# Two expert layers: how their last rows are added, branched past, normalised and stored, and where one weight bundle waits

## The chip, the core and the metric

One core of a Trainium2 chip runs the whole program. The metric is the device time of one execution in microseconds; the median of 3 executions counts. All values are f32; large products are made of fp32r halves (a value is cut into a high part and what is left of it, "hi" and "lo", and three products of halves are summed).

## What is computed

A first block (gated delta rule plus dilated attention, then a feed-forward layer) is followed by a second block of two layers, each of attention and a mixture of experts. S = 256 rows of D = 1024 values. What the change touches, from the reference:

```python
for i in range(DEPTH_2):                      # two layers
    mod = silu_c @ ada_w[i] + ada_b[i]        # modulation: shifts, scales and gates from c
    sh1, sc1, g1, sh2, sc2, g2 = [m[:, None, :] for m in jnp.split(mod, 6, axis=-1)]
    h = rms_norm(x, norm_mix_g[i]) * (1.0 + sc1) + sh1
    ...                                       # attention of the layer; x = x + g1 * y
    h = rms_norm(x, norm_ffn_g[i]) * (1.0 + sc2) + sh2
    x = x + g2 * grouped_moe(h, router_w, router_bias, moe_w_gate[i], moe_w_up[i], moe_w_down[i])
return x

def grouped_moe(...):                         # 16 experts, top 2 of one group of 4
    for e in range(N_EXPERTS):
        he = jax.nn.silu(t @ w_gate[e]) * (t @ w_up[e])
        out = out + gates[:, e:e + 1] * (he @ w_down[e])
```

## The kernel before, in words

The program is written by hand for each engine, with semaphores between them. The rows x (x_res) lie as 2 tiles (t) of 128 rows x 1024 columns; a half is 512 columns, one PSUM bank.

**An expert layer.** The experts go in 8 pairs (p). For a pair, up to 64 rows for each expert are gathered by a product with a 0/1 matrix; then come 4 gate units and 4 up units (`pair_up`, L1230), each with 1 MB of weights, SiLU on ScalarE (L1378), a product on VectorE (`hid_mul`, L1479), four transposes (L1303), a copy (`hid_copy`, L1482), and 4 down units (`pair_down`, L1240). VectorE scales the two result halves into o_f (`out_rows`, L1428), ScalarE copies them as fp32r into o_hi (`out_hi`, L1368), VectorE takes the difference o_lo (`out_lo`, L1433), and TensorE scatters: for each tile and half, sel_t times o_hi and o_lo into a bank (`scatter_mm`, L632), which VectorE adds to x (`add_rows`, L1464). The scatter of a pair runs within the next pair, behind its transposes. For pairs 0, 2, 4 and 6 it has only banks 0 and 1, so its third and fourth part wait until the first and second are added.

**The last pair** makes its down products by halves (`last_down_pe`): half 0 of all four units, then half 1; each half then goes through out_rows, out_hi, out_lo, scatter and add (`last_out_dve`, `last_scatter_pe`, `last_scatter_dve`).

**The overflow branch.** If an expert has more than 64 rows, further rounds run in a loop. Each engine loads a flag into a register (TENSOR_LOAD) and branches past the loops; in these runs they are skipped. The branch stands behind the last scatter on TensorE, behind the last add on VectorE.

**Between the layers.** In layer 0 ScalarE loads the Sqrt table, makes the high parts of two bundles of the next QKV weights (`splits`, L618), squares x with a row sum (L739) and takes the root (L708). VectorE makes the low parts (L622), the reciprocal (L757) and two scaled identities (`norm_apply`, L765). TensorE turns and scales the rows by 16 f32 products (`turn_pe`, L803); VectorE applies the modulation (`shift_dve`, L853), ScalarE and VectorE cut the result into a_hi (L844) and a_lo (L858), four pieces in order; then the QKV products run (L632), one weight bundle per piece of two column blocks.

**The end.** SP stores the two tiles of x, 512 KB each, when each is complete (L1761).

**Order of transfers.** SP issues weight loads in program order into a ring of 17 places (`PLACE_ORDER`); place 17 is made of last_place and grow. POOL issues the 48 bundles of the modulation weights (ada_w), each 1 MB with a place from a table (`ADA_PLACE`); TensorE multiplies them one by one (`ada_bundle`, L557). Ahead of layer 0's QKV products stand bundles 40, 41 and 42, with filler products (`busy`, L1207: f32 128x128 products whose result is not read) of 8, 5 and 0 behind them (`BUSY_MOD`).

## Time and profile before

| what | value |
|---|---|
| time, median of 3 runs | 1154.24 us (1153.57 to 1154.55) |
| profiled execution, its own time | 1153.23 us |
| its span, first to last instruction | 1151.3 us |
| TensorE busy | 1100.7 us (96%) |
| VectorE, ScalarE, GpSimd busy | 603.7, 423.7, 101.0 us |
| mean granted TensorE clock | 0.995 of full |

Times within the profile are microseconds from the start of the span. A row of the timeline has start, duration, engine, line, operation, out<-in and how many instructions were merged; in brackets stands how long the engine was idle ahead of it, and what released it. PE is TensorE's products, PEld its weight loads, DVE VectorE, ACT ScalarE. A plain f32 product leaves two records: the 17 fillers at the program's start (L1864) show as 34.

### The profile page before, as it was taken

Reading aid. Unit: us, or ns where it says so; the run is one execution under the profiler, and the core shown is the slowest. Engines: PE = TensorE matmul, PEld = TensorE weight load, DVE = VectorE, ACT = ScalarE, POOL = GpSimd, SP = SyncE. Lnnn points to the kernel's source line nnn. Section 1 sums busy time; section 2 is a strip of 40 time slices with the busy share of each in tenths; the row PEclk is TensorE's granted clock in tenths of the full one; section 3 lists DMA queues with packets and bytes.
Section 4 is the critical chain, followed back from the end, with each engine's and each line's share of the span. In section 5 each row is a group of like instructions: output and inputs, shape, how many; then the busy total and the mean of one; then the engine's idle time right before and its main releaser. Section 6 shows DMA issues by size and latency. Waiting matters only on the chain.

```text
span 1151.3 us, 17400 instructions
## 1 busy us (share of the span) xinstructions
PE 1100.7 (96%) x6870; PEld 744.2 (65%) x6870; DVE 603.7 (52%) x1164; ACT 423.7 (37%) x731; POOL 101.0 (9%) x193
## 2 busy tenths in 40 slices
PE   9999999999999999999999999987999999999986
PEld 9887667899999967777634434326888754343422
DVE  3588756767887765676423322327756522332223
ACT  6445434644444444474401202106547412020200
POOL 0211123111121120020000000002000100000000
PEclk9999999999999999999999999998999999999999
DMA  9987684997999878665899999996576789999995
GB/s 289 299 254 275 219 319 143 262 341 216 329 332 305 259 257 308 208 232 175 335 399 409 409 409 408 410 402 221 176 264 239 281 300 409 409 409 409 409 409 232
DMA packets 164910, 356.14 MB, mean 309 GB/s; under 512 B 10840, under 2 KB 79704, under 8 KB 164704
## 3 DMA queue, kind: packets, MB, share of 16 engines
q1 hardware_dynamic: 147792, 295.81, 71.0%
q0 software_dynamic: 17024, 59.26, 15.0%
q8 instruction: 50, 0.82, 0.3%
q14 instruction: 28, 0.23, 0.1%
q10 hardware_dynamic: 16, 0.02, 0.0%
HBM read 351.89 MB, written 7.36 MB: 312 GB/s over the span
## 4 chain that ended last, share of the span: by engine, by line
PE 77%; DMA 9%; DVE 7%; ACT 3%; SPq 2%; issue 1%; POOL 0%; POOLq 0%; DVEq 0%; ACTq 0%
PE bank L632 38%; PE bank L1230 15%; PE bank L1240 8%; DMA ering<-in_moe_w_up 3%; DMA work<-in_moe_w_up 3%; PE bank L1199 3%; PE bank L557 2%; DMA ering<-in_ada_w 1%; PE bank L803 1%; PE bank L937 1%; SPq L502 1%; DVE wlo L622 1%; PE bank L2020 1%; PE bank L1303 1%; PE bank L968 1%
## 5 line engine op out<-in xcount | busy, mean ns | idle before, releaser
L622 DVE TENSOR_TENSOR wlo<-wraw,whi 128x1024 fp32r<-128x1024 f32 x150 | 179.1, 1221 | 58.3 <-ACT whi L618 57.6
L618 ACT ACTIVATE whi<-wraw 128x1024 fp32r<-128x1024 f32 x150 | 153.8, 1052 | 57.1 <-PE bank L632 51.7
L632 PE MATMUL bank<-a_hi,whi 128*128 128x256 f32 x512 | 146.3, 286 | 0.4 <-DVE wlo L622 0.3
L632 PE MATMUL bank<-a_lo,whi 128*128 128x256 f32 x512 | 144.8, 283 | 0.0
L632 PE MATMUL bank<-a_hi,wlo 128*128 128x256 f32 x512 | 144.8, 283 | 0.0
L1230 PE MATMUL bank<-ering,work 128*64 128x512 f32 x528 | 118.5, 595 | 6.0 <-DMA ering<-in_moe_w_gate 4.3
L1479 DVE TENSOR_TENSOR work<-work,bank 128x512 f32<-128x512 f32 x16 | 11.0, 687 | 197.7 <-PE bank L1230 197.7
L1368 ACT ACTIVATE o_hi<-work 128x512 fp32r<-128x512 f32 x32 | 20.2, 631 | 231.5 <-DVE work L1428 231.1
L632 PE MATMUL bank<-whi,a_hi 128*128 128x512 f32 x256 | 104.1, 407 | 0.8 <-DVE wlo L622 0.8
L632 PEld LDWEIGHTS bank<-a_hi,whi 128*128 128x128 f32 x512 | 98.0, 191 | 9.5 <-issue 7.3
L632 PE MATMUL bank<-whi,a_lo 128*128 128x512 f32 x256 | 99.9, 390 | 0.0
L632 PE MATMUL bank<-wlo,a_hi 128*128 128x512 f32 x256 | 99.8, 390 | 0.0
L632 PEld LDWEIGHTS bank<-a_lo,whi 128*128 128x128 f32 x512 | 98.1, 192 | 0.7
L632 PEld LDWEIGHTS bank<-a_hi,wlo 128*128 128x128 f32 x512 | 98.1, 192 | 0.0
L1230 PEld LDWEIGHTS bank<-ering,work 128*64 128x64 f32 x528 | 36.8, 137 | 81.6 <-issue 69.3
L1428 DVE SCALAR_TENSOR_TENSOR work<-bank,sm,mrow 128x512 f32<-128x512 f32 x32 | 22.7, 747 | 87.6 <-PE bank L1240 87.6
L632 PEld LDWEIGHTS bank<-whi,a_hi 128*128 128x128 f32 x256 | 48.1, 188 | 16.5 <-issue 6.6
L1356 ACT ACTIVATE work<-bank,mcol 128x256 f32<-128x256 f32 x64 | 31.8, 561 | 70.5 <-PE bank L1199 70.5
L632 PEld LDWEIGHTS bank<-whi,a_lo 128*128 128x128 f32 x256 | 48.1, 188 | 10.3
L632 PEld LDWEIGHTS bank<-wlo,a_hi 128*128 128x128 f32 x256 | 48.2, 188 | 8.8 <-issue 0.2
L1240 PE MATMUL bank<-ering,work 128*64 128x512 f32 x240 | 53.5, 595 | 0.0
L1464 DVE TENSOR_TENSOR x_res<-x_res,bank 128x512 f32<-128x512 f32 x64 | 40.2, 680 | 9.0 <-PE bank L632 9.0
(349 smaller groups left out, 1931.4 us busy)
## 6 DMA issues: line engine op xcount, KB each, us to landing
ering<-in_moe_w_gate SPq DMA_DIRECT2D x36, 1024.0 KB, 18.5
ering<-in_moe_w_up SPq DMA_DIRECT2D x30, 1024.0 KB, 14.6
ering<-in_moe_w_down SPq DMA_DIRECT2D x30, 1024.0 KB, 18.4
work<-in_ada_w POOLq DMA_DIRECT2D x44, 512.0 KB, 7.5
ering<-in_ada_w POOLq DMA_DIRECT2D x38, 512.0 KB, 5.4
wraw<-in_w_in SPq DMA_DIRECT2D x28, 512.0 KB, 7.2
work<-in_moe_w_up SPq DMA_DIRECT2D x14, 1024.0 KB, 16.4
work<-in_moe_w_down SPq DMA_DIRECT2D x14, 1024.0 KB, 18.0
```

What stands on the lines that cost most here:

```text
L502: sp.dma_start(dst, src).then_inc(raw_in[c % RING], 16)
L557: mm = nc.tensor.matmul(psum[ADA_BANK[g]][32 * q:32 * q + 32, :], silc[:, k, :], ada_part(n, q // 2)[:, (q % 2) * HALF:(q % 2 + 1) * HALF] ...
L618: nc.scalar.activation(w_hi(c), wraw[:, c % RING, :], ACT.Copy).then_inc(w_hi_done, 1)
L622: nc.vector.tensor_tensor(w_lo(u[0]), wraw[:, u[0] % RING, :], w_hi(u[0]).bitcast(F32), ALU.subtract).then_inc(w_lo_done, 1)
L632: mm = nc.tensor.matmul(out_ap, l, r, start=first and n == 0, stop=last and n == len(terms) - 1)
L1199: mm = nc.tensor.matmul(bank[:, kk * S:kk * S + cols], part[:, t, pair_cols(2 * b + kk)], sel[:, t, 0:cols // PAIR_SLOTS, :], start=n == 1 ...
L1230: mm = nc.tensor.matmul(bank[rows, :], x_e[:, k, rows], eunit(r, e)[:, kk * HALF:(kk + 1) * HALF], start=first and kk == 0, stop=last and ...
L1240: mm = nc.tensor.matmul(psum[4 + half][rows, :], hid_t[:, m % 4, rows], eunit(r, e)[:, half * HALF:(half + 1) * HALF], start=first, stop=last)
L1356: ins = nc.scalar.activation(xe[:, :, k, :], gather_bank(g, b)[:, kk * S:(kk + 1) * S].rearrange("p (a c) -> p a c", a=2), ACT.Identity, b ...
L1368: nc.scalar.activation(o_hi[:, cols], o_f[:, cols], ACT.Copy).then_inc(e_o_hi, 1)
L1428: return nc.vector.scalar_tensor_tensor(out=o_f[:, cols], in0=psum[4 + half][:, :], scalar=sm[:, M_GS:M_GS + 1], in1=mrow[:, 1, cols], op0 ...
L1464: return nc.vector.tensor_tensor(xs, xs, scatter_bank(p, n)[:, :], ALU.add)
```

## The change

It has six parts. (1) In the last two pairs the second half of each row tile is added in PSUM: within the last pair's up products, behind its second up unit, TensorE writes x's second halves into banks 6 and 7 by two f32 products with the identity, and the scatters of pairs 6 and 7 accumulate onto them. Pair 6 no longer waits for adds. VectorE copies the two banks into x at the end. (2) The last pair's second half is scattered from o_f by plain f32 products, without o_hi and o_lo. (3) The overflow branch stands ahead of the last pair's down products on TensorE, and ahead of the last `out_rows` on VectorE and `out_hi` on ScalarE. (4) Behind layer 0 the row sums are taken by halves, the second halves directly from the banks; one QKV bundle instead of two is cut ahead of them, three low parts are made within the modulation loop, and 10 fillers follow the last scatter on TensorE. (5) The result is stored in quarters of 256 KB, two by SP and two by ScalarE's queue. (6) Modulation bundle 42 goes into place 17 long before its use (POOL issues it behind `mod_spread(0)`), instead of the place in work.

```diff
+LAST_TWO = (PAIRS - 2, PAIRS - 1)
...
+BUSY_NEXT = 10
...
-ADA_TAIL = [0, 1, 2, 0, 1, 2, 11, 12, 14, 15, 13, 16, 2, 13, 16, 2]
+ADA_TAIL = [0, 1, 2, 0, 1, 2, 11, 12, 14, 15, 17, 16, 2, 13, 16, 2]
...
+ADA_EARLY = 42
...
+            return {11: 3, 12: 4, 13: 5, 14: 0, 15: 1, 16: 0, 17: 6}.get(ADA_PLACE[n], ADA_PLACE[n])
...
+            if at == 17:
+                return place_unit(LAST_PLACE, h)
...
+        def store_quarter(eng, n):
+
+            rows_, cols = slice(n % T * P, (n % T + 1) * P), slice(n // T * HALF, (n // T + 1) * HALF)
+            eng.wait_ge(x_done, X_AT["moe", 1] - X_W + n + 1)
+            eng.dma_start(out[0, rows_, cols], x[:, n % T, cols]).then_inc(x_rows, 16)
...
+        def norm_sums_of_halves(act):
+
+            for t in range(T):
+                act.wait_ge(x_done, X_AT["moe", 0] - X_W + t + 1)
+                nc.scalar.activation(hn[:, t, 0:HALF], x[:, t, 0:HALF], ACT.Square,
+                                     accum_out=sm[:, M_MS + t:M_MS + t + 1]).then_inc(nrm_sq, 1)
+            act.wait_ge(nrm_sq, 2 * 5 + 2)
+            nc.scalar.activation(sm[:, M_MS:M_MS + T], sm[:, M_MS:M_MS + T], ACT.Identity, bias=sm[:, M_EPS:M_EPS + 1],
+                                 scale=1.0 / D).then_inc(nrm_sq, 1)
+            for t in range(T):
+                act.wait_ge(e_sct, 4 * PAIRS - T + t + 1)
+                nc.scalar.activation(hn[:, t, HALF:D], psum[6 + t][:, :], ACT.Square,
+                                     accum_out=sm[:, M_SS + t:M_SS + t + 1]).then_inc(nrm_sq, 1)
+            act.wait_ge(nrm_sq, 2 * 5 + 5)
+            for t in range(T):
+                ins = nc.scalar.activation(sm[:, M_RS + t:M_RS + t + 1], sm[:, M_SS + t:M_SS + t + 1], ACT.Sqrt,
+                                           bias=sm[:, M_MS + t:M_MS + t + 1], scale=1.0 / D)
+            ins.then_inc(nrm_rs, 1)
 
...
+                    behind(b)
...
+            if p in LAST_TWO:
+                return psum[(0, 6, 1, 7)[n]]
+            if p < 0 or p % 2:
                 return psum[(0, 1, 6, 7)[n]]
             return psum[n % 2]
 
         def scatter_mm(p, n):
 
             t, half = n // 2, n % 2
+            on_rows = p in LAST_TWO and half == 1
             return products(scatter_bank(p, n)[:, :], [(sel_t[:, t, :], part[:, half * HALF:(half + 1) * HALF])
-                                                       for part in (o_hi, o_lo)], True, True)
+                                                       for part in (o_hi, o_lo)], not on_rows, not on_rows)
+
+        def rows_into_banks():
+
+            for t in range(T):
+                mm = nc.tensor.matmul(psum[6 + t][:, :], ident, x[:, t, HALF:D], start=True, stop=False)
+            return mm
+
+        def split_rows(l, p, half):
+
+            return 2 * turn_of(l, p) - l + half + 1
 
         def scatter_pe(pe, l, p, part):
 
             q = turn_of(l, p)
             if part == 0:
-                pe.wait_ge(e_o_lo, 2 * (q + 1))
+                pe.wait_ge(e_o_lo, split_rows(l, p, 1))
                 pe.wait_ge(e_sel_t, q + 1)
             for n in (2 * part, 2 * part + 1):
-                if part and p % 2 == 0:
+                if part and p % 2 == 0 and p not in LAST_TWO:
                     pe.wait_ge(x_done, X_AT["wo", l] + X_W * p + n - 1)
                 scatter_mm(p, n).then_inc(e_sct, 1)
...
+                    if p == PAIRS - 1 and kind == 1 and j == 1:
+                        pe.wait_ge(x_done, X_AT["wo", l] + X_W * (PAIRS - 2))
+                        rows_into_banks()
...
             q = turn_of(l, PAIRS - 1)
             pe.wait_ge(e_sel_t, q + 1)
-            for half in range(2):
-                pe.wait_ge(e_o_lo, 2 * q + half + 1)
-                for t in range(T):
-                    scatter_mm(PAIRS - 1, 2 * t + half).then_inc(e_sct, 1)
+            pe.wait_ge(x_done, X_AT["moe", l] - X_W)
+            pe.wait_ge(e_o_lo, split_rows(l, PAIRS - 1, 0))
+            for t in range(T):
+                scatter_mm(PAIRS - 1, 2 * t).then_inc(e_sct, 1)
+            pe.wait_ge(e_o, 2 * (q + 1))
+            for t in range(T):
+                nc.tensor.matmul(psum[6 + t][:, :], sel_t[:, t, :].bitcast(F32), o_f[:, HALF:D], start=False,
+                                 stop=True).then_inc(e_sct, 1)
...
-                dve.wait_ge(e_o_hi, 2 * q + half + 1)
-                out_lo(half).then_inc(e_o_lo, 1)
+                if half == 0:
+                    dve.wait_ge(e_o_hi, split_rows(l, PAIRS - 1, 0))
+                    out_lo(0).then_inc(e_o_lo, 1)
...
-            for n in range(4):
+            for n in range(0, 4, 2 if p in LAST_TWO else 1):
                 dve.wait_ge(e_sct, 4 * turn_of(l, p) + n + 1)
-                add_rows(p, n).then_inc(x_done, 1)
-
-        def last_scatter_dve(dve, l):
-
-            for i, n in enumerate((0, 2, 1, 3)):
-                dve.wait_ge(e_sct, 4 * turn_of(l, PAIRS - 1) + i + 1)
-                add_rows(PAIRS - 1, n).then_inc(x_done, 1)
+                add_rows(p, n).then_inc(x_done, 2 if p in LAST_TWO else 1)
+
+        def rows_from_bank(t):
+            return nc.vector.tensor_copy(x[:, t, HALF:D], psum[6 + t][:, :])
+
+        def last_scatter_dve(dve, l, splits_dve):
+
+            for t in range(T):
+                dve.wait_ge(e_sct, 4 * turn_of(l, PAIRS - 1) + t + 1)
+                add_rows(PAIRS - 1, 2 * t).then_inc(x_done, 1)
+            if l == 0:
+                splits_dve(U_QKV[1] + 1)
+            for t in range(T):
+                if l == 0:
+
+                    dve.wait_ge(nrm_sq, 2 * 5 + 4 + t)
+                else:
+                    dve.wait_ge(e_sct, 4 * turn_of(l, PAIRS - 1) + T + t + 1)
+                rows_from_bank(t).then_inc(x_done, 1)
 
...
-                            sp.wait_ge(mod_rows, 256)
+                            sp.wait_ge(ada_used, ada_count(ADA_EARLY))
...
-            for t in range(T):
-                sp.wait_ge(x_done, X_AT["moe", 1] - (T - 1 - t))
-                sp.dma_start(out[0, t * P:(t + 1) * P, :], x[:, t, :]).then_inc(x_rows, 16)
-            sp.wait_ge(x_rows, 16 * (T + 1))
+            for n in range(0, 2 * T, 2):
+                store_quarter(sp, n)
+            sp.wait_ge(x_rows, 16 * (2 * T + 1))
...
+            pool.wait_ge(mod_rows, 256)
+            load_ada(pool, ADA_EARLY)
...
+                if l == 1:
+                    busy(psum[2], BUSY_NEXT)
...
-                last_scatter_pe(pe, l)
                 over = pe.value_load(ints[0:1, 0:1], min_val=0, max_val=1)
                 with pe.If(over > 0):
-                    pe.drain().then_inc(ov_pe[l], OV_PE)
-                    for r in range(1, ROUNDS):
-                        with pe.Fori(0, PAIRS) as i:
-                            over_pe(pe, l, r, i)
+                    over_begin_pe(pe, l)
+                    with pe.Fori(0, PAIRS * (ROUNDS - 1)) as i:
+                        over_pe(pe, l, 1, i)
                     over_end(pe, l)
+                    rows_into_banks()
+                last_down_pe(pe, l)
+                last_scatter_pe(pe, l)
 
 
 
...
-                out_hi(act, l, PAIRS - 1)
...
+                out_hi(act, l, PAIRS - 1, (0,))
+                if l == 0:
+
                     act.wait_ge(e_used, TURNS)
-                    splits(U_QKV[1] + 2)
+                    splits(U_QKV[1] + 1)
+            for n in range(1, 2 * T, 2):
+                store_quarter(act, n)
...
-                shift_dve(dve, 3 + 3 * l, mcol[:, l, 0:8], mcol[:, l, 8:16])
+                shift_dve(dve, 3 + 3 * l, mcol[:, l, 0:8], mcol[:, l, 8:16],
+                          lambda b: splits(U_QKV[1] + b + 1) if l == 1 and b < 4 else None)
...
-                last_out_dve(dve, l)
-                last_scatter_dve(dve, l)
                 dve.wait_ge(table_done, l + 1)
                 over = dve.value_load(ints[0:1, 0:1], min_val=0, max_val=1)
                 with dve.If(over > 0):
...
                     over_end(dve, l)
-                if l == 0:
-                    splits(U_QKV[1] + 2)
+                last_out_dve(dve, l)
+                last_scatter_dve(dve, l, splits)
```

What moves on the engines, as the instruction lists show it. o_hi and o_lo are the fp32r halves of a pair's result, sel_t the scatter matrix, work the f32 result o_f or weights. TensorE at the end of the second expert layer, before, behind the last down product:

```order
L1240 MATMUL bank<-a_raw_56,work 64x512 [waits first_in]
L1240 MATMUL bank<-a_raw_56,work 64x512
L632 MATMUL bank<-o_hi,sel_t 128x512 [waits e_o_lo,e_sel_t]
L632 MATMUL bank<-o_lo,sel_t 128x512
L632 MATMUL bank<-o_hi,sel_t 128x512
L632 MATMUL bank<-o_lo,sel_t 128x512
L632 MATMUL bank<-o_hi,sel_t 128x512 [waits e_o_lo]
L632 MATMUL bank<-o_lo,sel_t 128x512
L632 MATMUL bank<-o_hi,sel_t 128x512
L632 MATMUL bank<-o_lo,sel_t 128x512
L2263 TENSOR_LOAD ints
```

After, from the last unit's down products to the program's end:

```order
L1270 MATMUL bank<-work 64x512 x4
L1270 MATMUL bank<-a_raw_55,work 64x512 x2
L1270 MATMUL bank<-a_raw_56,work 64x512 [waits first_in]
L1270 MATMUL bank<-a_raw_56,work 64x512
L643 MATMUL bank<-o_hi,sel_t 128x512 [waits e_o_lo,x_done,e_sel_t]
L643 MATMUL bank<-o_lo,sel_t 128x512
L643 MATMUL bank<-o_hi,sel_t 128x512
L643 MATMUL bank<-o_lo,sel_t 128x512
L1395 MATMUL bank<-work,sel_t 128x512 [waits e_o]
```

Four fp32r products and the flag's load are gone from behind the last down products, and two plain f32 products stand there. The flag's load now stands ahead of the down products, here from within pair 6's scatter on (L1317 turns sel_g; the x_res row behind the branch is skipped):

```order
L643 MATMUL bank<-o_hi,sel_t 128x512
L643 MATMUL bank<-o_lo,sel_t 128x512
L643 MATMUL bank<-o_hi,sel_t 128x512
L643 MATMUL bank<-o_lo,sel_t 128x512
L643 MATMUL bank<-o_hi,sel_t 128x512
L643 MATMUL bank<-o_lo,sel_t 128x512
L1317 MATMUL bank<-con,work 128x128 [waits e_sel_t,e_sel_g]
L1317 MATMUL bank<-con,work 128x128
L2368 TENSOR_LOAD ints [waits e_o,e_hid_t]
L2368 ISA x2
L2369 COMPARE_AND_BRANCH
```

VectorE behind layer 0, from the branch to the second piece of the modulation, before:

```order
L3034 UNCONDITIONAL_BRANCH [waits ov_dve0]
L622 TENSOR_TENSOR wlo<-wraw,whi 128x1024 [waits w_hi_done] x2
L757 RECIPROCAL sm<-sm 128x2 [waits nrm_rs]
L765 TENSOR_SCALAR hn<-con,sm 128x128 [waits nrm_inv]
L765 TENSOR_SCALAR hn<-con,sm 128x128
L853 TENSOR_SCALAR work<-bank,mcol 128x256 [waits tr_done]
L853 TENSOR_SCALAR work<-bank,mcol 128x256
L853 TENSOR_SCALAR work<-bank,mcol 128x256 [waits tr_done]
L853 TENSOR_SCALAR work<-bank,mcol 128x256
L858 TENSOR_TENSOR a_lo<-work,a_hi 128x512 [waits a_hi_done]
L853 TENSOR_SCALAR work<-bank,mcol 128x256 [waits tr_done]
```

The same stretch after, from the last pair's `out_rows` of half 1 on:

```order
L1477 SCALAR_TENSOR_TENSOR work<-bank,sm,mrow 128x512 [waits e_used]
L1514 TENSOR_TENSOR x_res<-x_res,bank 128x512 [waits e_sct] x2
L633 TENSOR_TENSOR wlo<-wraw,whi 128x1024 [waits w_hi_done]
L1523 COPY x_res<-bank 128x512 [waits nrm_sq] x2
L786 RECIPROCAL sm<-sm 128x2 [waits nrm_rs]
L794 TENSOR_SCALAR hn<-con,sm 128x128 [waits nrm_inv]
L794 TENSOR_SCALAR hn<-con,sm 128x128
L882 TENSOR_SCALAR work<-bank,mcol 128x256 [waits tr_done]
L882 TENSOR_SCALAR work<-bank,mcol 128x256
L882 TENSOR_SCALAR work<-bank,mcol 128x256 [waits tr_done]
L882 TENSOR_SCALAR work<-bank,mcol 128x256
L887 TENSOR_TENSOR a_lo<-work,a_hi 128x512 [waits a_hi_done]
```

The branch has moved up, out of this stretch; two of four adds became copies that wait for ScalarE's squares (nrm_sq); one of two low parts (wlo) went into the modulation loop.

## Rows read from the trace of the kernel before

**Rows 1.** The page: the chain that ended last, shares by engine.

```profile
PE 77%; DMA 9%; DVE 7%; ACT 3%; SPq 2%; issue 1%; POOL 0%; POOLq 0%; DVEq 0%; ACTq 0%
```

**Rows 2.** Timeline, layer 0's end, TensorE's products.

```profile
763.03 1.94 PE L1230 MATMUL bank<-work 128*64 128x512 f32 x8 [0.62 <-DMA work<-in_moe_w_up]
...
767.79 0.50 PE L632 MATMUL bank<-o_hi,sel_t 128*128 128x512 f32 x1 [0.46 <-DVE x_res L1464]
...
769.26 1.94 PE L1240 MATMUL bank<-work 128*64 128x512 f32 x8
```

**Rows 3.** The same timeline, a later window.

```profile
776.51 0.50 PE L632 MATMUL bank<-o_hi,sel_t 128*128 128x512 f32 x1
...
777.32 0.40 PE L632 MATMUL bank<-o_lo,sel_t 128*128 128x512 f32 x1
...
785.02 5.33 PE L803 MATMUL bank<-hn,x_res 128*128 128x128 f32 x32 [5.00 <-DVE hn L765]
```

**Rows 4.** Timeline, layer 0's last down products, TensorE's weight loads.

```profile
770.70 0.14 PEld L1240 LDWEIGHTS bank<-a_raw,work 128*64 128x64 f32 x2 [0.38 <-DMA a_raw<-in_moe_w_down]
...
772.07 0.20 PEld L1240 LDWEIGHTS bank<-a_raw,work 128*64 128x64 f32 x4 [0.89 <-DMA a_raw<-in_moe_w_down]
```

**Rows 5.** Timeline, layer 0's end, VectorE.

```profile
776.63 0.75 DVE L1428 SCALAR_TENSOR_TENSOR work<-bank,sm,mrow 128x512 f32<-128x512 f32 x1 [1.22 <-PE bank L1240]
...
778.69 2.47 DVE L1464 TENSOR_TENSOR x_res<-x_res,bank 128x512 f32<-128x512 f32 x4
781.52 2.36 DVE L622 TENSOR_TENSOR wlo<-wraw,whi 128x1024 fp32r<-128x1024 f32 x2 [0.36 <-issue]
784.19 0.17 DVE L757 RECIPROCAL sm<-sm 128x2 f32<-128x2 f32 x1 [0.31 <-ACT sm L708]
```

**Rows 6.** Timeline, layer 0's end, ScalarE.

```profile
777.41 0.63 ACT L1368 ACTIVATE o_hi<-work 128x512 fp32r<-128x512 f32 x1 [2.73 <-DVE work L1428]
778.36 1.28 ACT L724 ACT_TABLE_LOAD   x1 [0.32 <-issue]
...
779.76 1.99 ACT L618 ACTIVATE whi<-wraw 128x1024 fp32r<-128x1024 f32 x2
781.65 1.04 ACT L739 ACTIVATE hn<-x_res 128x1024 f32<-128x1024 f32 x1
```

**Rows 7.** Windows of 1 us: length, busy, count, granted clock, DMA.

```profile
781.00:782.00 1.00, 0.00 (x0) 0.00 (x0) 0.64 (x2) 1.00 (x2) 0.00 (x0) 0.69 0.00 0
...
788.00:789.00 1.00, 1.00 (x10) 1.00 (x10) 0.50 (x2) 0.63 (x1) 1.00 (x3) 0.90 0.90 189
```

**Rows 8.** TensorE's groups by shape: busy us, mean ns, idle before.

```profile
L1207 PE MATMUL bank<-con 128*128 128x128 f32 x196 | 24.4, 278 | 0.0
...
L1937 PE MATMUL bank<-work,con 128*128 128x512 f32 x8 | 3.7, 602 | 1.2 <-ACT work L2356 1.2
```

**Rows 9.** Timeline ahead of layer 0's QKV, all engines.

```profile
411.70 1.07 PE L557 MATMUL bank<-a_raw,silc 128*32 128x512 f32 x8 [0.73 <-DMA a_raw<-in_ada_w]
...
417.98 3.84 PE L803 MATMUL bank<-hn,x_res 128*128 128x128 f32 x32
419.18 1.90 DVE L853 TENSOR_SCALAR work<-bank,mcol 128x256 f32<-128x256 f32 x4 [3.34 <-PE bank L803]
```

**Rows 10.** Timeline, the program's end, all engines.

```profile
1142.14 0.75 DVE L1428 SCALAR_TENSOR_TENSOR work<-bank,sm,mrow 128x512 f32<-128x512 f32 x1 [1.23 <-PE bank L1240]
...
1144.20 2.47 DVE L1464 TENSOR_TENSOR x_res<-x_res,bank 128x512 f32<-128x512 f32 x4
...
1146.10 1.58 SPq L1761 DMA_DIRECT2D out_x<-x_res  x2
```

**Rows 11.** DMA issues: count, KB each, median us to landing.

```profile
out_x<-x_res SPq DMA_DIRECT2D x2, 512.0 KB, 3.7
```

**Rows 12.** Timeline, SP's queue around its own overflow branch.

```profile
757.26 2.36 SPq L1737 DMA_DIRECT2D a_raw<-in_moe_w_down  x1
761.09 58.15 SPq L502 DMA_DIRECT2D wraw<-in_b_w_qkv  x19
```

More of the change, by code:

```diff
@@ L477, in build_program @@
         sil_c = sem("sil_c")
-        ada_in = [sem(f"ada_in{b}") for b in range(6)]
+        ada_in = [sem(f"ada_in{b}") for b in range(7)]
         ada_used, grow_done, acol_done = sem("ada_used"), sem("grow_done"), sem("acol_done")
@@ L728, in norm_sums @@
         def norm_sums(act, n, xs):
-            if n != 5:
-                warm(ACT.Sqrt)
+            warm(ACT.Sqrt)
             for t in range(T):
@@ L845, in shift_hi, with shift_dve @@
                                      ACT.Copy).then_inc(a_hi_done, 1)
-        def shift_dve(dve, turn, gain, shift):
+        def shift_dve(dve, turn, gain, shift, behind):
             for b in range(5):
@@ L1359, in gathered_act, with out_hi @@
                 ins.then_inc(e_x, 1)
-        def out_hi(act, l, p):
-            for half in range(2):
+        def out_hi(act, l, p, halves=range(2)):
+            for half in halves:
                 cols = slice(half * HALF, (half + 1) * HALF)
@@ L1445, in out_lo_dve @@
             for half in range(2):
-                dve.wait_ge(e_o_hi, 2 * turn_of(l, p) + half + 1)
+                dve.wait_ge(e_o_hi, split_rows(l, p, half))
                 out_lo(half).then_inc(e_o_lo, 1)
@@ L1511, in ov, with over_begin_pe, over_begin_act, over_begin_dve @@
             return per * i + per * PAIRS * (r - 1) + k
+        def over_begin_pe(pe, l):
+            nothing = ident[0:32, 64:P]
+            for t in range(T):
+                for rows_ in BLOCKS:
+                    nc.tensor.matmul(psum[6 + t][rows_, :], nothing, x[0:32, t, HALF:D], start=False, stop=True)
+            for j in range(4):
+                r = LOADS * (PAIRS - 1) + 8 + j
+                pe.wait_ge(e_in[r % PLACES], eturn(l, r))
+                if j == 3:
+                    pe.wait_ge(first_in, 16 * (3 + l))
+                mm = pair_down(pe, r, j == 0, j == 3)
+            mm.then_inc(ov_pe[l], OV_PE - 1)
+            pe.wait_ge(ov_dve[l], OV_DVE - 1)
+            for n in range(4):
+                mm = scatter_mm(-1, n)
+            mm.then_inc(ov_pe[l], 1)
+        def over_begin_act(act, l):
+            act.wait_ge(ov_dve[l], OV_DVE - 2)
+            nc.scalar.activation(o_hi[:, :], o_f[:, :], ACT.Copy).then_inc(ov_act[l], OV_ACT)
+        def over_begin_dve(dve, l):
+            dve.wait_ge(ov_pe[l], OV_PE - 1)
+            for t in range(T):
+                rows_from_bank(t)
+            dve.wait_ge(e_sel_t, turn_of(l, PAIRS - 1) + 1)
+            out_rows(0)
+            out_rows(1).then_inc(ov_dve[l], OV_DVE - 2)
+            dve.wait_ge(ov_act[l], OV_ACT)
+            out_lo(0)
+            out_lo(1).then_inc(ov_dve[l], 1)
+            dve.wait_ge(ov_pe[l], OV_PE)
+            for n in range(4):
+                ins = add_rows(-1, n)
+            ins.then_inc(ov_dve[l], 1)
         def over_sp(sp, l, r, i):
@@ L1529, in over_pe @@
         def over_pe(pe, l, r, i):
-            pe.wait_ge(ov_dve[l], ov(OV_DVE, 2, r, i))
+            pe.wait_ge(ov_dve[l], ov(OV_DVE, OV_DVE + 2, r, i))
             for b in range(4):
@@ L1539, in over_pe @@
             mm.then_inc(ov_pe[l], 1)
-            pe.wait_ge(ov_dve[l], ov(OV_DVE, 3, r, i))
+            pe.wait_ge(ov_dve[l], ov(OV_DVE, OV_DVE + 3, r, i))
             for k in range(4):
@@ L1546, in over_pe @@
             tr.then_inc(ov_pe[l], 1)
-            pe.wait_ge(ov_act[l], ov(OV_ACT, 3, r, i))
+            pe.wait_ge(ov_act[l], ov(OV_ACT, OV_ACT + 3, r, i))
             for j in range(4):
@@ L1550, in over_pe @@
             mm.then_inc(ov_pe[l], 1)
-            pe.wait_ge(ov_dve[l], ov(OV_DVE, 6, r, i))
+            pe.wait_ge(ov_dve[l], ov(OV_DVE, OV_DVE + 6, r, i))
             for n in range(4):
@@ L1583, in over_dve @@
             out_rows(1).then_inc(ov_dve[l], 1)
-            dve.wait_ge(ov_act[l], ov(OV_ACT, 4, r, i))
+            dve.wait_ge(ov_act[l], ov(OV_ACT, OV_ACT + 4, r, i))
             out_lo(0)
@@ L1590, in over_dve @@
             ins.then_inc(ov_dve[l], 1)
+        OV_LAST = OV_DVE * (PAIRS * (ROUNDS - 1) + 1) + 1
         def over_end(eng, l):
-            eng.wait_ge(ov_dve[l], OV_DVE * PAIRS * (ROUNDS - 1))
+            eng.wait_ge(ov_dve[l], OV_LAST)
         block = ctx.enter_context(nc.Block())
@@ L1826, in _ @@
             pool.wait_ge(w_used, up_unit(U_FFN, FF_STEPS - 1) + 1)
-            for n in range(ADA_FFN, ADA_MOD):
+            for n in range(ADA_FFN, ADA_EARLY):
                 load_ada(pool, n)
@@ L2430, in _ @@
             for l in range(2):
-                norm_sums(act, 3 + 2 * l, X_AT["lnf"] if l == 0 else X_AT["moe", 0])
+                if l == 0:
+                    norm_sums(act, 3, X_AT["lnf"])
+                else:
+                    norm_sums_of_halves(act)
                 if l == 1:
@@ L2524, in _ @@
                 with act.If(over > 0):
-                    for r in range(1, ROUNDS):
-                        with act.Fori(0, PAIRS) as i:
-                            over_act(act, l, r, i)
+                    over_begin_act(act, l)
+                    with act.Fori(0, PAIRS * (ROUNDS - 1)) as i:
+                        over_act(act, l, 1, i)
                     over_end(act, l)
@@ L3034, in _ @@
                 with dve.If(over > 0):
+                    over_begin_dve(dve, l)
                     for r in range(1, ROUNDS):
```

19 lines of the change are left out of this document (9 added, 10 removed).

## The prediction, made before the result was known

> **What bounds the kernel now.** I read the page's chain first: 77% of it is TensorE's products, 9% DMA, 7% VectorE, 3% ScalarE [rows 1]. So TensorE's time counts almost everywhere, and what a change can win lies in the few places where TensorE waits. I then went through the timeline at the ends of both expert layers.
>
> At layer 0's end TensorE stands still for 5.00 us ahead of the turning products [rows 3]. The reader should see what fills them: VectorE's `out_rows` of half 1 at 776.63, four adds from 778.69 (2.47 us, 0.62 each), reciprocal at 784.19 [rows 5]; on ScalarE the table load, two high parts (1.99 us) and only then the squares of 1.04 us each [rows 6]. The windows show a second loss: the granted clock falls during 781 to 782 and is back during 788 to 789 [rows 7], and the 32 turning records take 5.33 us at 785.02 [rows 3], where the same 32 at full clock took 3.84 us [rows 9]. At the program's end the last add is done at 1144.20 + 2.47 = 1146.67, the stores are issued from 1146.10 on [rows 10], and the span ends at 1151.3.
>
> Ahead of both ends the weights arrive just in time. TensorE waits 0.62 us ahead of the last up unit [rows 2], the two units ahead of it alike, and in the down products the first half of the last unit arrives at 772.07 after 0.89 us of idle weight loading [rows 4].
>
> **The change part by part**, in layer 0's clock times.
>
> (a) x's second halves into banks 6 and 7. The nearest row for a plain f32 product of 128 x 512 is L1937: 8 records, so 4 products, in 3.7 us [rows 8]; 0.92 each, less 0.06 when the pipeline is full. Two take 1.7 to 1.85 us. Behind them come two gaps of 0.62 us, each with some 0.17 us of a product's tail that the next can cover: 1.6 us of cover. Up ends 0.1 us later, at worst 0.6 (if no tail is covered). It is not free elsewhere: down products start later by that, see (b).
>
> (b) Pair 6's scatter loses its two waits for adds: 0.46 us idle at 767.79 [rows 2] and a shorter one behind it, 0.8 us together. So TensorE would reach the down products at about 768.5 instead of 769.26 [rows 2]. That wins nothing itself: the last unit's first half still arrives at 772.07 [rows 4], and three products of 0.86 us from 769.26 end at 771.84. But it is the cover for (c): 0.8 + 0.2 - 0.1 = 0.9 us.
>
> (c) The flag's load and branch ahead of the down products. TensorE's own is hidden in the 5.00 us, so its price is bounded by others: ScalarE from the start of its last o_hi to the next start 778.36 - 777.41 = 0.95 us [rows 6]; VectorE from the start of its fourth add (778.69 + 3 x 0.62 = 780.55) to 781.52, 0.97 us [rows 5]; SP from 757.26 + 2.36 = 759.62 to 761.09, 1.47 us [rows 12]. Against 0.9 us of cover, 0 to 0.6 us per layer is exposed. I take 0, because on TensorE's queue up to ten products are still to be executed when the sequencer reaches the load. Behind the branch are queued the down products, and everyone waits for these. VectorE's and ScalarE's branches go to where they wait for TensorE anyway.
>
> By that, half 0 and half 1 of the down products end when they did: out_rows of half 1 starts at 776.63 and ends at 777.38 [rows 5].
>
> (d) Layer 0's end. TensorE starts its fourth fp32r scatter product at 777.32 [rows 3] and is free at about 777.55; the two f32 products end at 778.5 and 779.4. VectorE's two adds of first halves end at 778.0 and 778.7. ScalarE: table already loaded; one high part 776.63 to 777.63 (half of 1.99); two squares of 512 columns, priced at the 0.63 us of o_hi [rows 6], end 779.4; scaling 0.35 (an estimate from the 0.46 us that lie between 781.65 + 2 x 1.04 and the reciprocal at 784.19 [rows 5, 6]), 779.75; two squares from the banks, 781.05; the roots 0.4, 781.45. VectorE's second copy waits for the second of these squares and takes 0.6 to 0.7 us: 781.75. The reciprocal starts at 781.8, not 784.19: 2.4 us. TensorE starts 0.83 us behind it as before (784.19 to 785.02), at 782.6.
>
> (e) Ten fillers. 196 records are 98 products in 24.4 us, 0.25 us each [rows 8]: 779.3 to 781.8, clear of 782.6, so they cost nothing. They leave 0.8 us of idle instead of the 1.3 us and more behind which the clock fell [rows 3, 7]. The turning takes 3.84 instead of 5.33 us: 1.5 us. Bounds 0 and 1.5.
>
> (f) Three low parts within the modulation loop. Modulation begins 1.20 us behind the turning's start (417.98 to 419.18) and takes 0.95 us a piece [rows 9]; with a_lo (0.62 as an add) and a low part (half of 2.36 [rows 5]) VectorE needs 2.75 us a piece. TensorE needs for a bundle 12 fp32r products: 3 pitches lie between 776.51 and 777.32 [rows 3], 0.23 to 0.27 each, 2.8 to 3.2 us. The two just match, so I take 0; bound 1.2 (one low part exposed).
>
> Layer 0: 2.4 + 1.5 = 3.9 us (bounds 0.5 and 4.3).
>
> (g) The program's end. out_rows of half 1 ends at 1142.14 + 0.75 = 1142.89 [rows 10]. TensorE's f32 products end, by the offsets of (d), at 1144.0 and 1144.9; the second copy ends at 1145.65, where the fourth add ended at 1146.67: 1.0 us. The stores: from the last add to the span's end are 4.6 us, in which two transfers of 512 KB follow each other. 512 KB take 1.37 us (770.70 to 772.07 [rows 4]), a quarter 0.69. After, three quarters are issued from 1143.5 on and are through; the last needs 0.69 instead of up to 2.74 us. That is 2.05 at best and 0.7 at worst (only a smaller last store, other things queued); I take 1.4. The median landing of 3.7 us [rows 11] leaves room for that. ScalarE's queue for two stores has no row near; I take SP's price.
>
> End: 1.0 + 1.4 = 2.4 us (bounds 1.7 and 3.0).
>
> (h) Bundle 42 in place 17. TensorE waits 0.73 us for bundle 40 at 411.70 [rows 9]; from there 40, 8 fillers, 41, 5 fillers and 42 run without a gap to 417.98. Bundle 42's transfer is issued behind both others, so 40 arrives as before, and the fillers stay: 0 us, at best 0.7. Its early transfer moves 1 MB into a stretch with no wait for it.
>
> Between the layers nothing swallows the 3.9 us: QKV and attention run on TensorE, and the weight stream of the second expert layer is released by TensorE's own uses.
>
> Sum: 3.9 + 2.4 = 6.3 us. The profiled execution took 1153.23 us with a span of 1151.3; I expect 1146.9 and 1145.0. The median of the runs is 1.0 us above the profiled one, so 1154.24 - 6.3 = 1147.9 us.
>
> **The rivals.**
> - Layer 0 gives half: the clock falls all the same, or low parts hold up the first bundles. For: 0.8 us of idle is near 1.3, and the match in (f) has no room. Against: the fillers run until then. 3.9 becomes 1.9: 1149.9 us.
> - TensorE's branch costs what SP's did or more, without a fall of the clock: 0.6 us per layer at 1.47, up to 1.3 at 2.2. 1149.1 to 1150.5 us.
> - Layer 0's gain is absorbed in front of the saturated weight stream of layer 1, and only the end is left: 1151.8 us. Against: that stream starts with TensorE's first products there.
> - More than I sum: bundle 40 earlier by 0.7 us, the stores by the full 2.05, no loss elsewhere: 6.3 + 0.7 + 0.6 = 7.6, 1146.6 us and a little below.
> - Slower: behind the taken branch TensorE has no instructions and waits for them. Nothing in the trace prices it for TensorE; above it is bounded by the 5.00 us in which the branch lay before [rows 3]. With a stall X the down products start X - 0.9 late, and as idle of 1.3 us lowered the clock, 1.5 us come on top, twice: at 5.0 us that is 11.2 us, 1159.1 us. It decides from X = 2.55 us on, where 2 x (2.55 - 0.9 + 1.5) = 6.3. Against it: three engines skipped their branches in 0.95 to 1.47 us. [...] The rows of the other engines show no such stall in what they skipped.
>
> **How the numbers follow.** The forecast 0.60, with its own range 1146.8 to 1149.0; layer 0 at half 0.14; branch exposed 0.08; absorbed 0.05; more than summed 0.07; slower 0.06. I predict 1147.9 us; 8 times in 10 it lies between 1145.9 and 1151.0, which leaves out absorption, the slow case and the tails. 0.2%, or 2.3 us, is about what a measurement can tell from no change: faster needs less than 1151.9. Faster 0.89, same 0.05, slower 0.06.
>
> **What would show it.** In the changed trace: (c) the last down products of layer 0 start at about 769.3 or earlier in these times, with no idle of over 0.2 us behind the turning of sel_g; (d) TensorE's idle, fillers included, from the last scatter to the turning is about 3.2 us; (e) the turning takes 3.8 to 3.9 us and no window there has a clock under 1; (f) the first four QKV bundles show no idle over 0.3 us; (g) the last store's issue lies 1.0 us earlier and the span ends 3.2 us behind it, not 4.6. I am wrong if TensorE idles over 1.3 us ahead of the down products, if the clock falls, or if a transfer of bundle 42 or a store by ScalarE delays something that I hold for free.

## The result, and the profile after

The changed kernel takes 1159.18 us (median of 6 runs, 1157.66 to 1161.64), the kernel before in the same job 1154.07 us (6 runs). The ratio is 1.0048, 95% interval 1.0038 to 1.0058: 0.5% slower, where 0.5% faster was forecast. The profiled execution has a span of 1157.9 us, 6.6 us more than before.

The chain of work that ended last, from the changed kernel's page, and its last stretch in order of time (start, length, what):

```profile
PE 79%; DMA 8%; DVE 7%; ACT 3%; issue 2%; POOL 0%; POOLq 0%; SPq 0%; DVEq 0%; ACTq 0%
...
1136.73 0.22 PE bank L1317 x2
1136.95 4.94 issue
1141.90 9.99 PE bank L1270 x32
1151.89 1.13 PE bank L643 x4
1153.02 1.73 PE bank L1395 x4
1154.74 0.03 issue
1154.77 0.69 DVE x_res L1523
```

"issue" went from 1% [rows 1] to 2%: time in which TensorE waited for nothing that has a row. At layer 0's end the timeline of TensorE's products has the same hole:

```profile
769.04 0.38 PE L1317 MATMUL bank<-con,work 128*128 128x128 f32 x2
775.23 3.68 PE L1270 MATMUL bank<-work 128*64 128x512 f32 x8 [5.81 <-issue]
778.70 2.10 PE L1270 MATMUL bank<-a_raw,work 128*64 128x512 f32 x8
...
785.20 1.88 PE L1395 MATMUL bank<-work,sel_t 128*128 128x512 f32 x4
786.92 2.40 PE L1237 MATMUL bank<-con 128*128 128x128 f32 x20
789.97 3.81 PE L832 MATMUL bank<-hn,x_res 128*128 128x128 f32 x32 [0.66 <-DVE hn L794]
```

The down products, at 769.26 before [rows 2], start at 775.23 behind 5.81 us of idle, and the first eight records take 3.68 us where eight took 1.94 [rows 2]. The rest is as forecast: the turning takes 3.81 us, not 5.33 [rows 3], and waits 0.66 us, not 5.00. The windows (length, busy and count, granted clock, DMA share, GB/s) show both losses and what the memory does meanwhile:

```profile
769.00:775.00 6.00, 0.42 (x3) 0.78 1.05 389
775.00:779.00 4.00, 3.77 (x10) 0.50 1.06 388
...
1137.00:1142.00 5.00, 0.10 (x2) 0.90 0.59 220
1142.00:1148.00 6.00, 6.00 (x16) 0.52 0.01 3
```

By single windows the granted clock is 1.00 up to 772, 0.66 during 772 to 773 and 0.50 from 773 to 779; in layer 1 0.98 during 1140 to 1141 and 0.50 from 1141 to 1145. The timeline has no row of TensorE in the hole; the view of the branch's source line has one (operation, count, shortest/median/longest in ns, first and last start). First the changed kernel's flag load and branch, then those of the kernel before:

```profile
L2368 PEldq TENSOR_LOAD <-ints x2: 314/398/481, 768.1 to 1135.6; - x2
L2369 PEldq COMPARE_BRANCH  x2: 5546/5866/6185, 769.0 to 1136.3; - x2
```

```profile
L2263 PEldq TENSOR_LOAD <-ints x2: 311/402/493, 778.8 to 1144.3; - x2
...
L2264 PEldq COMPARE_BRANCH  x2: 3337/3338/3340, 779.7 to 1145.0; - x2
```

The load takes 0.31 to 0.48 us and runs under the products: it starts at 768.1, and the last scatter product at 768.80. The branch takes 6.19 us in layer 0 and 5.55 us in layer 1. And it took 3.34 us before, from 779.7 to 783.0, almost all of it inside the idle that [rows 3] shows: the price stood in the trace that the prediction was made from. In the changed kernel's windows of a quarter microsecond, a packet of instructions lies within the branch on queue 8, at 772.50 to 772.75 (packets, MB, share of the 16 DMA engines):

```profile
q8 instruction: 1, 0.02, 28.1%
```

A second one at 774.00 to 774.25, on queue 14, is not TensorE's: it follows VectorE's own branch by 3.8 us, stands in run 3 below too, where TensorE doesn't stall, and is missing there in runs 1 and 2, where VectorE has no branch.

### The profile page after: what moved, and what is told of

The parts are those of the page before. It is cut to its first block, busy times and chain, and to the rows that moved or that the text cites. A ratio compares the mean times of both kernels' runs of the same rounds, so it can differ in the third digit from the quotient of the medians.

```text
span 1157.9 us, 17458 instructions
## 1 busy us (share of the span) xinstructions
PE 1108.2 (96%) x6898; PEld 747.4 (65%) x6898; DVE 600.1 (52%) x1158; ACT 423.2 (37%) x735; POOL 101.4 (9%) x193
## 4 chain that ended last, share of the span: by engine, by line
PE 79%; DMA 8%; DVE 7%; ACT 3%; issue 2%; POOL 0%; POOLq 0%; SPq 0%; DVEq 0%; ACTq 0%
PE bank L643 40%; PE bank L1260 16%; PE bank L1270 8%; DMA ering<-in_moe_w_up 3%; DMA row<-in_moe_w_up 3%; PE bank L1229 3%; PE bank L562 2%; DMA ering<-in_ada_w 1%; PE bank L967 1%; PE bank L832 1%; DVE wlo L633 1%; PE bank L2124 1%; PE bank L1349 1%; PE bank L998 1%; DVE a_lo L863 1%
## 5 line engine op out<-in xcount | busy, mean ns | idle before, releaser
L643 PE MATMUL bank<-wtail,a_hi 128*128 128x512 f32 x128 | 40.7, 399 | 1.2 <-DVE wtail L633 0.7
```

Of the source, the lines that this page charges most:

```text
L643: mm = nc.tensor.matmul(out_ap, l, r, start=first and n == 0, stop=last and n == len(terms) - 1)
```

## The experiments

Theory A, an assumption that the runs are to test: behind the taken branch TensorE has no instructions, fetches them and stands still; the clock falls with it. Rivals: the flag's load is what stalls (B), any taken branch does (C), or something else in the change is slow (D).

**1. No branch.** The four engines' flag loads and branches are taken out; on TensorE:

```
                 for p in range(PAIRS):
                     pair_pe(pe, l, p)
-                over = pe.value_load(ints[0:1, 0:1], min_val=0, max_val=1)
-                with pe.If(over > 0):
-                    ...
                 last_down_pe(pe, l)
```

> The changed kernel with the flag's load and the overflow branch left out on all four engines (the overflow rounds are not computed). Theory A, TensorE stalls behind the taken branch and its clock falls with it: both stalls (5.81 and 4.94 us) go, the down products run at full clock again (9.03 and 9.99 us become 7.1), so 1159.2 - 7.7 - 7.8 = 1143.7 us; as some of layer 0's delay was taken up by layer 1's weight stream already, 1144 to 1147 us. Theory B, the loss comes from the rest of the change (f32 products, low parts, stores) or from the memory traffic: over 1155 us, and the down products still start late.

Measured: 1145.68 us, ratio 0.9936 (0.9920 to 0.9953). Span 1142.9 us. TensorE's timeline in that run:

```profile
768.50 0.38 PE L1317 MATMUL bank<-con,work 128*128 128x128 f32 x2
768.81 1.94 PE L1270 MATMUL bank<-work 128*64 128x512 f32 x8
...
772.12 1.08 PE L1270 MATMUL bank<-a_raw,work 128*64 128x512 f32 x4 [0.29 <-DMA a_raw<-in_moe_w_down]
...
782.36 3.81 PE L832 MATMUL bank<-hn,x_res 128*128 128x128 f32 x32 [0.64 <-DVE hn L794]
```

No idle ahead of the down products, and a granted clock of 1.00 from 768.5 to 776.5 and in layer 1 from 1129 to 1137. D falls: with the branches gone the rest of the change gains 7.3 us, where 6.3 were forecast.

**2. The load alone.** As 1, but `over = pe.value_load(...)` stays on TensorE.

> As the kernel without a branch, but TensorE still loads the flag to a register ahead of the down products and doesn't branch. If the stall is the instructions that the taken branch must wait for, TensorE idles under 0.7 us there and the time is within 1 us of the kernel without a branch. If the stall is the load (TensorE's queue must run dry, the read of on-chip memory and its way back), the idle is 4 us and more and the time 1155 us or above.

Measured: 1146.24 us, ratio 0.9937 (0.9921 to 0.9954), indistinguishable from 1. The load takes 0.31 and 0.48 us and starts at 768.6 in layer 0, under the scatter products (the last starts at 769.27); the down products start at 769.82, without idle. B falls.

**3. A short jump.** The whole kernel, TensorE's body cut to one product:

```
                 with pe.If(over > 0):
-                    over_begin_pe(pe, l)
-                    ...
+                    busy(psum[0], 1)
```

> The changed kernel with TensorE's skipped body cut to one small product; the load, the compare and a taken branch stay, the other engines' branches whole (the overflow rounds are not computed). If the stall comes with the distance that is jumped: idle of 0.5 to 1.3 us ahead of the down products, full clock, at most 2 us above the kernel without a branch. If any taken branch on TensorE stalls: 4 us and more of idle, 1155 us or above.

Measured: 1146.59 us, ratio 0.9941 (0.9925 to 0.9958). The branch's line:

```profile
L2369 PEldq COMPARE_BRANCH  x2: 210/211/212, 768.9 to 1130.1; - x2
```

Here the taken branch over one product took 0.21 us, and the down products start at 769.27 without idle; in layer 0 the next packet on queue 8 comes 10.5 us behind it. C falls: it is where the jump leads.

**4. A hint.** The whole kernel, with an instruction at the start of the last pair that names the branch and its target. The branch is written by hand, as the hint must hang on it:

```
                 for p in range(PAIRS):
+                    if p == PAIRS - 1:
+                        hinted = pe.mark_branch_hint_location()
                     pair_pe(pe, l, p)
-                over = pe.value_load(ints[0:1, 0:1], min_val=0, max_val=1)
-                with pe.If(over > 0):
+                over = pe.to_reg(pe.value_load(ints[0:1, 0:1], min_val=0, max_val=1))
+                pe.br_lt(over, 1, on_true=f"past{l}", on_false=f"over{l}").branch_hint(hinted)
+                with nc.body(f"over{l}", valid_engines=[mybir.EngineType.PE]):
                     ...
+                    pe.br(f"past{l}")
+                nc.switch_bb(f"past{l}")
```

> The changed kernel whole, with one more instruction on TensorE at the start of the last pair that announces the branch's target (a branch prefetch hint). If the stall is a fetch of instructions that could have been made ahead: idle under 1.5 us ahead of the down products, 1144 to 1149 us. If the hint is dropped on the way or the stall is something else: 1158 to 1160 us, as the changed kernel.

Measured: 1144.87 us, ratio 0.9925 (0.9909 to 0.9942). The hint's and the branch's lines:

```profile
L2368 PEldq BRANCH_PREFETCH_HINT  x2: 41/46/52, 744.8 to 1104.5; - x2
L2371 PEldq COMPARE_BRANCH  x2: 344/356/367, 770.6 to 1130.1; - x2
```

With the hint 26 us ahead the same jump takes 0.34 and 0.37 us for 6.19 and 5.55, and TensorE doesn't idle: the down products start at 771.03 and 1130.66, right behind the turning of sel_g (0.38 us from 770.71 and 1130.35). A packet on queue 8 still comes 3.9 and 3.6 us behind the two branches (774.46 and 1133.76), but the down products run by then and nothing waits for it. In layer 1 one comes at 1110.87, 6.4 us behind the hint, that has no counterpart in the changed kernel; in layer 0 none can be told from the usual ones, so a fetch by the hint is not shown. The overflow branch stays whole, and the kernel is 0.75% faster than before.

**5. The hint too late.** As 4, with the hint directly ahead of the flag's load.

> The changed kernel with the hint, but given directly ahead of the flag's load instead of at the start of the last pair. Theory fetch: it takes 5.7 us from the branch to the first product behind it, and a hint that comes under 1 us ahead of the branch saves under 1 us of them: idle of 4 to 6 us, half clock, 1157 to 1160 us. If a hint works by itself wherever it stands: idle under 1 us, 1144 to 1147 us.

Measured: 1157.81 us, ratio 1.0041 (1.0027 to 1.0055).

```profile
L2368 PEldq BRANCH_PREFETCH_HINT  x2: 45/48/51, 767.7 to 1136.2; - x2
L2370 PEldq COMPARE_BRANCH  x2: 5406/5544/5681, 768.8 to 1137.0; - x2
```

A hint 1.1 us ahead in layer 0 and 0.8 us in layer 1 makes the branch 0.5 and 0.1 us shorter: less than it is ahead. From the late hint's start to the branch's end are 6.8 and 6.2 us. How far ahead is enough, between 1.1 and 26 us, was not tried.

**6. Three jumps for one.** The body cut into beginning, loop and end, each in a `with pe.If(over > 0):` of its own.

> The changed kernel with TensorE's one skipped body cut into three (beginning, loop, end), each behind a branch of its own on the same register. The sum of what is jumped is the same. If the stall is one fetch of the code behind the bodies: still 5 to 6 us of idle, as the three jumps follow each other within 1 us, 1158 to 1160 us. If only a single long jump stalls and three short ones find their targets fetched: idle under 2 us, 1145 to 1149 us. If each jump fetches anew: 8 us and more, 1163 us or above.

Measured: 1159.42 us, ratio 1.0061 (1.0044 to 1.0078). The three branches:

```profile
L2369 PEldq COMPARE_BRANCH  x2: 318/333/348, 768.6 to 1137.2; - x2
L2371 PEldq COMPARE_BRANCH  x2: 4342/5102/5862, 769.0 to 1137.6; - x2
L2374 PEldq COMPARE_BRANCH  x2: 213/216/220, 774.9 to 1142.0; - x2
```

Only the jump over the loop pays (5.86 us in layer 0, 4.34 in layer 1). Cutting the jump up gains nothing.

**7. The branch late.** The changed kernel, TensorE's load, branch and body behind `last_scatter_pe(pe, l)`.

> The changed kernel with TensorE's flag load, branch and body moved behind its last scatter products, where the kernel before had them (so the overflow rounds would read the wrong state; the flag is 0 here). The down products start at once. The taken branch then lies ahead of the fillers and the turning products. If the stall is 5 us and more wherever the branch stands, TensorE is free at about 779.5, stands still to about 784.5 and more, the 20 filler records come behind it, and the turning starts at 787 in these times instead of 782.4; nothing follows in layer 1: about 4.5 us above the kernel without a branch less what layer 1's weight stream takes up, 1148 to 1151 us. If the stall needs the down products behind it, the turning starts at 782.4 and the time is 1144 to 1147 us.

Measured: 1149.31 us, ratio 0.9962 (0.9949 to 0.9975), between 1 and the changed kernel.

```profile
776.85 1.88 PE L1395 MATMUL bank<-work,sel_t 128*128 128x512 f32 x4
781.37 4.12 PE L1237 MATMUL bank<-con 128*128 128x128 f32 x20 [2.65 <-issue]
785.34 3.74 PE L832 MATMUL bank<-hn,x_res 128*128 128x128 f32 x32
```

```profile
L2371 PEldq COMPARE_BRANCH  x2: 342/2040/3737, 777.6 to 1141.5; - x2
```

In layer 0 the branch takes 3.74 us, 2.65 of them in sight, and the fillers behind it take 4.12 us for 2.40 (mean granted clock 0.57 from 781.37 to 785.34). The turning starts 8.49 us behind the f32 products instead of 4.75 in run 1. Near what was expected, for less: I had put the stall at 5 us anywhere, it is 3.74 here. In layer 1 the same jump costs 0.34 us without a hint.

**8. The branch early, alone.** The kernel before with TensorE's load, branch and its old body ahead of `last_down_pe(pe, l)`, nothing else changed.

> The kernel before with one part of the change alone: TensorE's flag load and branch (its own old body, 3 rounds of 66 rows) stand ahead of the last down products. If the branch's place is what costs: down products start 5 to 6 us late in both layers and the first ones run at half clock; in the changed kernel that was 7.1 us to the down products' end in layer 0 and 7.7 us in layer 1. Sum 14.8 less about 1 us that layer 1's weight stream takes up: 1165 to 1168 us. If the stall needs the rest of the change: 1153 to 1157 us.

Measured: 1168.27 us, ratio 1.0134 (1.0117 to 1.0151), 15.2 us slower. The place alone costs this; the rest of the change is not needed for it. The branch takes 6.19 us in layer 0 and 4.21 in layer 1. The body that it skips has three loops where the changed kernel's has one, and layer 0's 6.19 us are the same: the longer jump costs no more.

```profile
775.55 3.68 PE L1240 MATMUL bank<-work 128*64 128x512 f32 x8 [6.36 <-issue]
```

**9. The hint in the kernel before.** The edit of 4 in `before`, branch in its old place.

> The kernel before with the hint on TensorE at the start of the last pair, branch in its old place. In the kernel before, the 5.00 us of idle ahead of the turning held the instruction packets at 780.5 and 782.0, and VectorE's hn came last. If the fetch was hidden under VectorE's and ScalarE's chain: same time as before, within 1 us, turning still starts 0.8 us behind the reciprocal. If the fetch was part of what held the turning back: 1 to 3 us faster.

Measured: 1153.19 us (11 runs), ratio 1.0000 (0.9991 to 1.0010). The branch fell from 3.34 us to 0.35 and 0.37, and nothing else moved:

```profile
L2266 PEldq COMPARE_BRANCH  x2: 351/362/374, 785.5 to 1150.5; - x2
```

TensorE still idles 5.00 us ahead of the turning. There the branch was hidden whole, as the prediction had it. (The profiled execution was an outlier, 5.6 us later from its first 210 us on; its durations stand.)

**10. Parts of the rest**, each taken out of the hinted kernel (4). First bundle 42 back in place 13 (`ADA_TAIL` with 13 for 17, its load behind 41's):

> The changed kernel with the hint, and bundle 42 back in its old place, loaded behind 40 and 41. In the runs with bundle 42 in place 17 TensorE waited 1.1 to 1.9 us for bundle 40 (0.73 us before), in the hinted one its clock fell in the fillers behind that. If the early transfer is the cause: the wait is 0.7 us again, no fall, the turning of layer 0's QKV starts at about 418.0 instead of 420.8, and the time is 0.5 to 2.5 us lower than with the hint alone (1142.5 to 1144.5 us). If it is the spread of one transfer from run to run: within 0.5 us of it, and waits of 0.7 to 1.9 us with no system.

Measured: 1144.22 us, ratio 0.9922 (0.9908 to 0.9935); 0.7 us under run 4, inside both intervals. TensorE waited 0.69 us for bundle 40. But over all profiles place 17 had waits of 0.62 to 1.91 us (ten), place 13 of 0.69 to 1.35 us (four). An effect of place 17 is not shown; if there is one, it is under 1 us.

Then without the ten fillers (`busy(psum[2], BUSY_NEXT)` taken out):

> The changed kernel with the hint, without the ten fillers ahead of layer 1's turning products. If they hold the clock: the granted clock falls in the idle of about 3 us, the turning takes 5.3 instead of 3.8 us, and the time is up to 1.5 us higher; since layer 1's weight stream ends the wait ahead of the last pairs, less of it is left at the end (0 to 1.5 us above 1144.9). If the clock does not fall in 3 us of idle: the turning takes 3.8 us, same time.

Measured: 1146.66 us, ratio 0.9940 (0.9927 to 0.9954), 1.8 us above run 4; the two intervals overlap, so the size is read from the trace.

```profile
782.48 5.17 PE L832 MATMUL bank<-hn,x_res 128*128 128x128 f32 x32 [2.88 <-DVE hn L794]
```

The granted clock is 1.00 up to 781, 0.96 during 781 to 782 and 0.50 from 782 to 785, behind 2.88 us of idle, and the turning takes 5.17 for 3.81 us: the fillers are worth 1.4 us.

Last, two stores of 512 KB on SP as before, in place of the four quarters:

> The changed kernel with the hint, with the result stored in two rows' halves of 512 KB by SP as before instead of four quarters on two queues. From the last copy's end to the span's end 4.6 us (as before) instead of 2.5: about 2.1 us higher, 1146.5 to 1147.5 us. If the stores' size did not matter: under 0.5 us.

Measured: 1145.80 us, ratio 0.9935 (0.9921 to 0.9948), 0.9 us above run 4 and not the 2.1 expected. From the last copy's end (1138.90 + 0.69) to the span's end (1143.1) are 3.5 us; with quarters 2.5 (run 1: 1139.71 + 0.69 to 1142.9), before 4.6. Each quarter lands in 2.1 us, a half here in 2.9, before in 3.7 [rows 11]. So the smaller stores give 1.0 us of the 2.1 (in the traces; the two runs' intervals overlap). The other 1.1 us are gained with halves too. The stores' own lines, of before and then of this run, show where over half of that lies: SP's issue of the second store took 0.98 us before (1.15 in run 9) and 0.36 here. Why it is shorter here was not tested.

```profile
L1761 SPq DMA_DIRECT2D out_x<-x_res x2: 360/670/980, 1146.1 to 1146.7; - x2
...
L1864 SPq DMA_DIRECT2D out_x<-x_res x2: 356/358/359, 1138.8 to 1139.6; - x2
```

## Why the prediction was wrong

**The step that failed is (c)**, "The flag's load and branch ahead of the down products": "TensorE's own is hidden in the 5.00 us, so its price is bounded by others", and "I take 0". The others' branches record 0.04 to 0.07 us, before and after; SP's too, which skips three loops of its own, so the others' price says nothing of TensorE's. Why theirs stay short was not tested. TensorE's recorded 3.34 us before and 5.55 to 6.19 us after. The error was made twice. The price was taken from other engines although TensorE's own branch has a row in the trace of before; only the timeline doesn't print it. And the rival "Slower" was told with "Nothing in the trace prices it for TensorE" and given 0.06. From the load's start at 778.8 to the branch's end at 779.7 + 3.34 are 4.2 us, above the 2.55 us from which that rival decides. Its formula then gives 2 x (4.2 - 0.9 + 1.5) = 9.6 us, so 1147.9 + 9.6 = 1157.5 us; measured were 1159.2. The stall behind the taken branch, the place and the fall of the clock (to 0.50) were those of the rival, which at 5.0 us named 1159.1. That it comes so near is partly luck: the stall depends on the place (3.34 us there, 6.19 and 5.55 here), and the clock's price, put at 1.5 us a layer, was 1.2 and 2.25.

What the runs show of the cause is this: the branch takes 0.21 us over one product and 5.55 to 6.19 us over the whole body in the same place, with a packet of instructions on queue 8 inside, and 0.34 and 0.37 us with a hint 26 us ahead. That it waits for a fetch is what these three suggest. The prediction set the stall aside because the other engines' rows showed none.

**The size of it in the changed kernel.** Against run 1 the span is 15.0 us longer. Layer 0: 5.81 us of idle, and from the first down product to the scatter 8.94 us (775.23 to 784.17) for 7.75 in run 1, 7.0 us together. Layer 1, of the same two kinds: 4.94 us of idle, then 9.92 us (1141.90 to 1151.82) for 7.67, 7.2 us together. Of the missing 0.8 us TensorE was 0.5 late already when it came to layer 0's end (769.04 for 768.50); the rest arose between the layers' ends.

**The rest held**, read in run 1, where (c) costs nothing:
- (a), (b): the down products start at 768.81, forecast about 768.5. The last half arrives at 772.12, as before.
- (d): the reciprocal runs at 781.54, forecast 781.8; the turning starts at 782.36, forecast 782.6.
- (e): 3.81 us of turning, and a granted clock of 1.00 from 782 to 787; the run without fillers shows that they are why.
- (f): nothing lost: the first 96 records of QKV take 22.04 us, 22.01 before. Layer 0's end gains 4.2 us (790.35 to 786.18), forecast 3.9.
- (g): the copies gain 1.0 us as forecast (from the down products' end at 1136.84 to the last copy's end 3.6 us, before 4.6). The stores gain 2.1 us, not 1.4. That this meets the bound "2.05 at best" is chance: what was priced, the smaller last store, gave 1.0 us (run 10), and for the other 1.1 us the sum had no term.
- (h): not distinguishable from 0.

Sum 4.2 + 1.0 + 2.1 = 7.3 us, forecast 6.3; the medians of run 1 and of before in its job differ by 1152.97 - 1145.68 = 7.3. The spans differ by 8.4 us, since the profiled execution of before had a delay of its own: three weight loads on SP's queue at 1050.42 took 8.50 us there and 7.28 to 7.31 us in all twelve other profiles of the experiments and in the changed kernel's.

```profile
1050.42 8.50 SPq L1739 DMA_DIRECT2D ering<-in_moe_w_down  x3
```

## What to carry to other kernels

Before moving a branch, look up its own instruction by its line. Here TensorE's branch had 3.34 us in the view of its line and no row in the timeline; it was not free, it was hidden in 5.00 us of idle. Without a hint the jump over the overflow body, or over its loop alone, took TensorE 3.34 to 6.19 us in nine of ten cases, and 0.34 us in the tenth. Two ways out were measured: leave it where the engine waits anyway (in the kernel before a hint gained nothing, ratio 1.0000), or announce it with a prefetch hint well ahead (26 us ahead the branch took 0.34 and 0.37 us; 1.1 and 0.8 us ahead it took 5.68 and 5.41). Price it by that engine's own branch, not by those of other engines (0.04 to 0.07 us here), and don't carry that price to another place unchanged: here it was 3.34 us where the branch stood and up to 6.19 where it went.

## What the runs showed of the hardware that was not expected

TensorE's branch over the body or its loop took 0.34 to 6.19 us by its place. Each case without a hint, with the time from the branch's start to the packet on queue 8, and what the memory did meanwhile:

| kernel, layer | branch, us | to the packet, us | weight stream meanwhile |
|---|---|---|---|
| changed, 0 | 6.19 | 3.7 | full, 379 to 403 GB/s |
| before with the branch early, 0 | 6.19 | 3.7 | full, 383 to 391 GB/s |
| split (loop), 0 | 5.86 | 3.4 | full, 383 to 393 GB/s |
| changed, 1 | 5.55 | 3.1 | 367 to 393 GB/s to 1139, then 264 and 74 |
| split (loop), 1 | 4.34 | 1.9 | 391 to 401 GB/s to 1139, then 320 and 209 |
| before with the branch early, 1 | 4.21 | 1.8 | 381 to 389 GB/s to 1144, then 246 and 86 |
| late, 0 | 3.74 | 1.1 | 389 GB/s to 778, then 320 to 168 |
| before, 0 | 3.34 | 1.0 | 270 to 111 GB/s, then none |
| before, 1 | 3.34 | 1.0 | none |
| late, 1 | 0.34 | behind the branch's end | none |

The packet itself takes 1.0 to 1.3 us (its share of the 16 DMA engines in a window of a quarter microsecond, 23.9 to 32.6%, is that much time of one), and from its end to the branch's end it is 1.3 to 1.4 us in every one of these stalls. So the spread lies ahead of the packet. That fits a fetch that queues behind the kernel's own transfers, but one row goes against it: in "late, 0" the stream was full (389 GB/s) when the branch began, and the packet came after 1.1 us. No run varied the traffic alone, and the kernels' code stands at different places, so the cause of the spread is argued and not shown. Why the late branch of layer 1 took 0.34 us stays open too. It alone of these rows had a packet shortly ahead, 7.7 us before it began; in the others the last one lay 20 to 31 us back. From the packet on queue 8 to TensorE's first product behind the branch it is 2.5 to 2.9 us wherever TensorE waits for nothing else.
